# A two-layer hybrid decoder trunk on one core: the norms' sum of squares in fp32r, and another order of the first units of each phase

## What is computed

```python
def rmsnorm(x, w, eps=NORM_EPS):
    y = xf * lax.rsqrt(jnp.mean(xf * xf, axis=-1, keepdims=True) + eps)
    return y * w
def swiglu(x, w_gate, w_up, w_down):
    return (jax.nn.silu(x @ w_gate) * (x @ w_up)) @ w_down
# layer 0: x += mixer_ab (RG-LRU branch and RWKV-7 branch); layer 1: x += mixer_c (gated delta rule)
z = h @ w_in                                        # mixer_c: 32 blocks of 128 columns and 16 more
qkv = jax.nn.silu(causal_dwconv(z[..., :3 * W], conv_w))
beta = jax.nn.sigmoid(z[..., 4 * W:4 * W + DN_HEADS]); alpha = z[..., 4 * W + DN_HEADS:]
```

## Time and profile before

| | us |
|---|---|
| three runs | 2139.29, 2138.38, 2140.01; median 2139.29 |
| the profiled execution, its own time | 2139.55 |
| its span (first to last instruction) | 2137.8 |

### The profile page before, as it was taken

The page is one execution under the profiler, slowest core; times in us unless marked ns, Lnnn a source line. Parts: engine busy times, 40 slices in busy tenths (PEclk is TensorE's granted clock), DMA queues, the critical chain, the costliest instruction groups (busy, mean ns, idle before and its releaser), DMA issues. The chain is left out here.

```text
span 2137.8 us, 33198 instructions
## 1 busy us (share of the span) xinstructions
PE 2082.0 (97%) x13332; PEld 1707.7 (80%) x13332; DVE 1126.3 (53%) x1451; ACT 778.0 (36%) x1175; POOL 167.6 (8%) x120
## 2 busy tenths in 40 slices
PE   8999999999789999999999999999999999999998
PEld 6888888777758888888888888877888878888886
DVE  5444444678756444434444443468776665444322
ACT  4333222483334333322332232245665443223221
POOL 2000011002302000001000001101110120000010
PEclk9999999999999999999999999999999999999999
DMA  4222332320102322332222233221111122222321
GB/s 179 93 94 98 114 102 70 105 75 15 38 27 88 106 91 97 109 109 87 79 98 98 96 109 100 89 71 60 51 41 50 56 79 93 98 96 92 117 95 53
DMA packets 48265, 182.65 MB, mean 85 GB/s; under 512 B 6320, under 2 KB 6576, under 8 KB 48048
## 3 DMA queue, kind: packets, MB, share of 16 engines
q1 hardware_dynamic: 48176, 181.39, 25.6%
HBM read 179.27 MB, written 2.10 MB: 85 GB/s over the span
## 5 line engine op out<-in xcount | busy, mean ns | idle before, releaser
L586 PE MATMUL banks<-H,WS 128*128 128x512 f32 x1840 | 730.8, 397 | 10.4 <-DVE H L1967 7.8
L588 PE MATMUL banks<-H,WS 128*128 128x512 f32 x1840 | 718.0, 390 | 0.0
L587 PE MATMUL banks<-H,WS 128*128 128x512 f32 x1840 | 717.9, 390 | 0.0
L1259 ACT ACTIVATE WS<-RAW 128x1024 fp32r<-128x1024 f32 (+1 forms) x310 | 349.3, 1127 | 937.7 <-PE banks L588 933.7
L1883 DVE TENSOR_TENSOR WS<-RAW,WS 128x1024 fp32r<-128x1024 f32 (+1 forms) x310 | 407.1, 1313 | 234.8 <-ACT WS L1259 234.6
L586 PEld LDWEIGHTS banks<-H,WS 128*128 128x128 f32 x1840 | 346.3, 188 | 90.3 <-DVE WS L1883 10.6
L588 PEld LDWEIGHTS banks<-H,WS 128*128 128x128 f32 x1840 | 346.2, 188 | 72.8
L587 PEld LDWEIGHTS banks<-H,WS 128*128 128x128 f32 x1840 | 346.4, 188 | 71.1 <-issue 2.4
L586 PE MATMUL banks<-A,WS 128*128 128x512 f32 x704 | 273.9, 389 | 0.0
L587 PE MATMUL banks<-A,WS 128*128 128x512 f32 x704 | 273.9, 389 | 0.0
L588 PE MATMUL banks<-A,WS 128*128 128x512 f32 x704 | 273.9, 389 | 0.0
(11 more groups left out here) (374 smaller groups left out, 1662.7 us busy)
## 6 DMA issues: line engine op xcount, KB each, us to landing
RAW<-in_w_gate SPq DMA_DIRECT2D x88, 512.0 KB, 3.3
RAW<-in_w_up SPq DMA_DIRECT2D x88, 512.0 KB, 3.3
RAW<-in_w_down SPq DMA_DIRECT2D x64, 704.0 KB, 4.0
RAW<-in_c_in SPq DMA_DIRECT2D x32, 512.0 KB, 3.3
RAW<-in_ab_in SPq DMA_DIRECT2D x22, 512.0 KB, 3.2
RAW<-in_ab_out SPq DMA_DIRECT2D x8, 512.0 KB, 3.6
RAW<-in_c_out SPq DMA_DIRECT2D x8, 512.0 KB, 3.3
X<-in_x SPq DMA_DIRECT2D x4, 512.0 KB, 6.7
```

Of the source, the lines that this page charges most:

```text
L586: pe.matmul(bank[:, :], WS[:, 0, s, cols], upper, start=first and j == 0, stop=False)
L587: pe.matmul(bank[:, :], WS[:, 0, s, cols], lower, start=False, stop=False)
L588: mm = pe.matmul(bank[:, :], WS[:, 1, s, cols], upper, start=False, stop=last and j == len(rows) - 1)
L1259: act.activation(WS[:, 0, c % SPLIT, 0:cols], RAW[:, c % RING, 0:cols], ACT.Copy).then_inc(hi_ready, 1)
```

## The change

It does three things. The sum of squares of norms 1 to 5 is completed on GpSimd (the eighth square too, once H's last row is done), split by ScalarE and VectorE into fp32r parts SUM_HI (in RSTD's place) and SUM_LO, and multiplied with ones in fp32r. `first_two` ends unit 0 after rows 0 and 1 of unit 1, and does the norm behind row 5 of unit 1; in the delta mixer the norm moves from behind slot 3 to behind slot 5. And the delta mixer's units 0 to 3 get banks 0 to 3, so that unit 4 is the first to wait for a read.

```diff
+        def c_bank(t):
+            return BANK[t if t < 4 else t % 2]
+        ONES_R = at("ONES_R", SPARE_AT + 3 * P + 20 * TT * HEADS, [P, P], F32R)
+        SUM_LO = at("SUM_LO", SPARE_AT + 4 * P + 20 * TT * HEADS, [P, SEQ], F32R)
+        SUM_HI = at("SUM_HI", RSTD_AT, [P, SEQ], F32R)
+        def odd_sums(n):
+            return 4 * n - 1 if n else 0
...
             def first_two(phase, banks):
-                for k in range(2):
-                    unit(banks[k], c + k, 0, H_PARTS, range(KB - 1), True, False, norm=n, done=False)
-                for k in range(2):
-                    unit(banks[k], c + k, 0, H_PARTS, [KB - 1], False, True, norm=n, at_col=KB - 1)
-                    if k == 0:
-                        norm_sum(n)
+                unit(banks[0], c, 0, H_PARTS, range(KB - 1), True, False, norm=n, done=False)
+                unit(banks[1], c + 1, 0, H_PARTS, range(2), True, False, norm=n, done=False)
+                unit(banks[0], c, 0, H_PARTS, [KB - 1], False, True, norm=n, at_col=KB - 1)
+                unit(banks[1], c + 1, 0, H_PARTS, range(2, KB - 2), False, False, at_col=2, done=False)
+                norm_sum(n)
+                unit(banks[1], c + 1, 0, H_PARTS, range(KB - 2, KB), False, True, at_col=KB - 2)
...
             def norm_sum(n):
+                if n:
+                    pe.wait_ge(ones_split, 1)
+                    pe.wait_ge(sum_lo, n)
+                    pe.wait_ge(rms_ready, n)
+                    pe.matmul(SQ[:, :], ONES_R[:, :], SUM_HI[:, :], start=True, stop=False)
+                    pe.matmul(SQ[:, :], ONES_R[:, :], SUM_LO[:, :], start=False, stop=True).then_inc(sum_ready, 1)
+                    return
...
                     def slot():
-                        if k == 0 and t >= 2:
-                            pe.wait_ge(*c_z(t - 1))
-                        unit(BANK[t % 2], u0 + t, ...
+                        if k == 0 and t >= 4:
+                            pe.wait_ge(*c_z(t - 3 if t < 6 else t - 1))
+                        unit(c_bank(t), u0 + t, ...
...
-                        if g == 3:
+                        if g == 5:
                             norm_sum(n)
...
+            def sum_split(n):
+                act.wait_ge(acc_ready[1], odd_sums(n + 1))
+                last_use(act, plan[n - 1])
+                act.activation(SUM_HI[:, :], ACC[:, :], ACT.Copy).then_inc(sum_hi, 1)
             def root(n):
                 act.wait_ge(sum_ready, n + 1)
-                if n:
-                    last_use(act, plan[n - 1])
...
                 if base[phase]:
+                    if norm_of[phase] == 1:
+                        act.activation(ONES_R[:, :], con("ones"), ACT.Copy).then_inc(ones_split, 1)
+                    sum_split(norm_of[phase])
                     split_hi(base[phase] + 2, 0)
                 root(norm_of[phase])
...
                 residual(n, KB // 2 - 1, 0)
+                if 0 < n < n_norms - 1:
+                    pool.wait_ge(h_ready[1], KB // 2 * (n + 1))
+                    residual(n, KB // 2 - 1, 1)
...
             for phase in plan:
+                if base[phase]:
+                    vec.wait_ge(sum_hi, norm_of[phase])
+                    vec.tensor_tensor(SUM_LO[:, :], ACC[:, :], SUM_HI[:, :].bitcast(F32), ALU.subtract).then_inc(sum_lo, 1)
                 split_lo(base[phase] + 2, 0)
```

More of the change, by code:

```diff
@@ L432, in hybrid_trunk_kernel @@
         GATE_C = at("GATE_C", TMP_AT, [P, 4, SEQ])
+        ONES_R = at("ONES_R", SPARE_AT + 3 * P + 20 * TT * HEADS, [P, P], F32R)
+        SUM_LO = at("SUM_LO", SPARE_AT + 4 * P + 20 * TT * HEADS, [P, SEQ], F32R)
+        SUM_HI = at("SUM_HI", RSTD_AT, [P, SEQ], F32R)
+        ones_split, sum_hi, sum_lo = sem("ones_split"), sem("sum_hi"), sem("sum_lo")
+        def odd_sums(n):
+            return 4 * n - 1 if n else 0
         CT = at("CT", SPARE_AT, [P, KB, 2 * HEADS])
@@ L614, in norm_sum @@
             def norm_sum(n):
[L616 to L620, removed]
                 if n:
+                    pe.wait_ge(ones_split, 1)
+                    pe.wait_ge(sum_lo, n)
                     pe.wait_ge(rms_ready, n)
+                    pe.matmul(SQ[:, :], ONES_R[:, :], SUM_HI[:, :], start=True, stop=False)
+                    pe.matmul(SQ[:, :], ONES_R[:, :], SUM_LO[:, :], start=False, stop=True).then_inc(sum_ready, 1)
+                    return
+                pe.wait_ge(landed, 16)
+                pe.wait_ge(acc_ready[0], 4)
+                pe.wait_ge(acc_ready[1], 3)
+                pe.wait_ge(sq_ready[1], 4)
                 pe.matmul(SQ[:, :], con("ones"), ACC[:, :], start=True, stop=False)
@@ L965, in slot @@
                         t, k = divmod(next(dense), 4)
-                        if k == 0 and t >= 2:
-                            pe.wait_ge(*c_z(t - 1))
-                        unit(BANK[t % 2], u0 + t, 0, H_PARTS, (2 * k, 2 * k + 1), k == 0, k == 3, norm=n if t == 0 else None,
+                        if k == 0 and t >= 4:
+                            pe.wait_ge(*c_z(t - 3 if t < 6 else t - 1))
+                        unit(c_bank(t), u0 + t, 0, H_PARTS, (2 * k, 2 * k + 1), k == 0, k == 3, norm=n if t == 0 else None,
                              at_col=2 * k, done=k == 3)
@@ L1235, in _ @@
             pe.wait_ge(acc_ready[0], 4 * (n + 1))
-            pe.wait_ge(acc_ready[1], 3 * (n + 1))
+            pe.wait_ge(acc_ready[1], odd_sums(n) + 3)
             pe.wait_ge(rms_ready, n)
@@ L1264, in square @@
                     act.wait_ge(acc_ready[0], KB // 2 * n + i)
-                if j == 1 and fits(3 * n + i):
-                    act.wait_ge(acc_ready[1], 3 * n + i)
+                if j == 1 and fits(odd_sums(n) + i):
+                    act.wait_ge(acc_ready[1], odd_sums(n) + i)
                     if n:
@@ L1750, in residual @@
                 pool.wait_ge(sq_ready[j], KB // 2 * n + i + 1)
-                if j == 0 and fits(3 * n + i):
-                    pool.wait_ge(acc_ready[1], 3 * n + i)
+                if j == 0 and fits(odd_sums(n) + i):
+                    pool.wait_ge(acc_ready[1], odd_sums(n) + i)
                 if j == 1:
@@ L2314, in piece @@
                             vec.wait_ge(unit_done, u0 + t + 1)
-                            vec.tensor_tensor(pad[:, 3:3 + SEQ] if t < 24 else GATE_C[:, t % 4, :], BANK[t % 2][:, :], RSTD[:, :],
+                            vec.tensor_tensor(pad[:, 3:3 + SEQ] if t < 24 else GATE_C[:, t % 4, :], c_bank(t)[:, :], RSTD[:, :],
                                               ALU.mult).then_inc(c_z.sem, 1)
```

## The result

The changed kernel takes 2133.28 us (median of 11 runs, 2132.11 to 2135.47), the kernel before 2138.41 in the 11 runs beside it. The ratio is 0.9974, with a 95% interval of 0.9966 to 0.9982: faster by 5.6 us by the ratio, between 3.8 and 7.3, and by 5.1 us between the two medians. Forecast were 2133.4 and 5.9 less. The profiled execution took 2135.47 with a span of 2133.7.

A forecast was written before the change was run, and what follows sets the result against it. TensorE, busy for 97% of the span, was taken to bound the kernel. Four seams at 1.65 us less 0.7 lost at the delta mixer gave 5.9 us, so 2139.3 became 2133.4; range 2130.9 to 2136.8.

The forecast's parts named there:

- Part 1: Norms 1 to 5: fp32r products cut TensorE's time from 1.70 to 0.45 us each, with the sum's chain not late.
- Part 2: Four dense seams: unit 0 ending earlier lets unit 2's weights be split in time, removing 0.41 us of waiting each.
- what is late next: Dense seams: unit 3's low part, behind VectorE's reciprocal, stays in time; its cover grows from 0.36 to 1.3 us.
- The queues: First mixer's start: LW's clearing and unit 4's load come 5.4 to 6.3 us later, cover 2.3 us, cost nothing.
- Part 3: Delta mixer's start: square root 0.78 us later, TensorE waits 1.95 us before the tail, 0.7 us lost.
- Part 4: Delta mixer's four banks: zero gain, since the tail's 5.5 us already hide the wait they remove.
- (a): New idle time at the delta mixer also lowers the clock, costing 1.7 us: 2135.1; chance 0.2.
- (b): Delta mixer's tail doesn't wait because the sum's chain is faster than forecast: 2131.4; chance 0.07.
- (c): Dense seams: unit 0's earlier end buys nothing, the 0.41 us having another cause: 2135.0; chance 0.08.
- (d): The sum's new chain is late at all four dense seams, making the kernel slower: 2143.6; chance 0.04.
- (e): Lower clock, long GpSimd add and unit 4's load landing 2 us beyond its cover come together: 2138.0; chance 0.03.
- (f): Delta mixer: the square root doesn't follow the table load at once, so the tail waits longer; chance 0.02.

The follow-up runs named there:

- run 1: The changed kernel with `first_two` in its old order, so only the cheaper sum of squares and the delta mixer's changes remain: 2139.55 us, ratio 1.0001.
- run 2: The kernel before with only the new order of `first_two`, both fp32 norm products kept: 2137.00 us, ratio 0.9991.
- run 8: The changed kernel with GpSimd's clearing of LW moved ahead of the extra add: 2132.56 us, ratio 0.9972.
- run 4: The changed kernel with the split of the tail's weights (CTS) ahead of the root on ScalarE and the reciprocal on VectorE: 2129.70 us, ratio 0.9959.
- run 9: The changed kernel with the delta mixer's norm behind slot 3 again: 2133.55 us, ratio 0.997.
- run 3: The changed kernel with the old two banks and old wait in the delta mixer: 2133.37 us, ratio 0.9971.
- run 7: The changed kernel with the delta mixer's tail products behind slot 11 instead of 7, and two banks instead of four: 2133.95 us, ratio 0.9975.
- run 5: The changed kernel with the tail's weights split first and two banks for the delta mixer's first units: 2130.59 us, ratio 0.9961.

## Why the prediction was right

**The time** came out at 2133.28 against 2133.4, the step at 5.1 by the medians and 5.6 by the ratio against 5.9. Part of the near hit is luck: the kernel before was 0.9 lower in these runs than the median the sum stood on.

**Part 1** (1.70 becomes 0.45): 0.47 measured. Its chain: the add took 1.28 of the two bounds 1.27 and 2.21, since VectorE is idle beside it; the chain ended 7.12 after the start (1041.27 + 0.69), forecast 7.1. The Trainium skill, SBUF — State Buffer, "Who interferes with whom", says that GpSimd's reads contend with VectorE instructions that have two inputs in SBUF; this trace agrees: the line's median is 2.13, and the add that waits for VectorE's last H row, with VectorE idle beside it, takes 1.28.

**Part 2** (0.41 from unit 0's late end): run 1 shows the cause and run 2 the size, 0.36 to 0.41. What the text left out is that the two parts don't add: part 1 alone is worth nothing at a seam, as 12.94 against 12.92 shows. The step "what is late next" held: unit 3's cover is 1.36, forecast 1.3.

**The queues.** LW's clearing and the loads behind it came 5.4 us later, and unit 4 didn't wait (run 8).

**Part 3** was the step that mattered. Forecast: root 0.78 later, wait 1.95, loss 0.7. Measured: 0.78, 1.96, 0.69; and run 4 takes the wait away and gets 1.98 back. The reason held in the main (run 9): 0.59 of the 0.78 hang on ScalarE's chain and 0.19 on the later slot. The text had named both and given neither a size. The Trainium skill, ScalarE: Activation LUTs, "What ACT_TABLE_LOAD costs", has a drain of about 1.38 us with the load at every switch of tables. It did not appear: in run 9 the load starts 20 ns after the instruction in front of it ends, and the root follows the load after 10 ns.

**Part 4**: run 3 shows zero, run 7 where the banks would count.

**Rivals.** (a) is real but did not come: none of the four traces with this 1.8 us wait (the changed kernel, runs 1, 3 and 8) has a lower clock within 50 us behind it, and run 7, with 2.41, has. (b), (c) and (d) are ruled out by the rows and by run 1. (e) is too: there was no such clock, the add took 1.28, and unit 4 didn't wait. (f) is ruled out by the 10 ns.

**Where it was off.** The sum said 5.9 and the runs 5.1 to 5.6, with an interval that holds all three. In the two profiled executions the seams and the delta mixer give -6.0 (ab's dense units end 1.70 earlier after its start, FFN 1 and 2 1.68 each, the mixer +0.68, and FFN 3 1.64: its unit 2 starts 11.36 after the start instead of 12.91, and the next product 0.09 closer). The remaining +1.9 lies in FFN 0 (+0.71), in ab behind its dense units (+0.6) and at the end (+0.6), where no part of the change works. The last two go with a lower clock in the profile of the changed kernel: 0.81 against 0.87 from 618 to 645, and 0.70 against 0.76 in the last 17.7 and 17.8 us. That the medians' missing 0.8 has this cause was not tested.

## What to carry to other kernels

Cheaper work on the bounding engine pays only if whatever it covered is not just in time: look at what ends in the last tenths of a us before that engine arrives, since here a 0.14 us cover turned into a 1.96 us wait. Of two parts one can be worth nothing on its own and the other a third of the whole, so test them together too before dropping one. An operation that doesn't need a late result, as the split of the tail's weights, should not be queued behind it: run 4 gained 1.98 us at that place.

## What was not expected of the hardware

The runs of one kernel scatter by 3 us or more (2132.11 to 2135.47 for the changed one), and its mean granted clock goes with it: 0.996 or 0.995 in the executions of 2132.1 to 2132.7, 0.994 in those of 2133.3 to 2134.0, 0.993 in the two above 2135. The stretches at the lower clock mostly fall in parts where TensorE has idle times, but not in the same ones in each execution: of the twelve profiles of this case, eight have a mean granted clock of 0.91 from 1452 to 1472, and the four of runs 2, 4, 5 and 7 have 1.00 there, with TensorE busy for 17 to 18 of the 20 us in all. In the same twelve the RWKV part takes 65.6 to 66.3 us in the four with such a stretch in it and 63.3 to 64.5 in the eight without. So some 2 us of a difference between two single profiles of this kernel can be chance.
